# Binary search for top-k limits with the sign inside the candidate, and all masks made ahead of the attention

## The chip, the cores and the metric

The kernel runs on one core of a Trainium2 chip. The metric is the device time of one execution in microseconds (us). The engines are TensorE (PE), VectorE (DVE), ScalarE (ACT), GpSimd (POOL), and SyncE (SP), which here issues the DMAs.

## The reference, cut to what matters

The program is one step of a two-layer decoder trunk for 1024 prompt tokens and 32 sample tokens (8 sequences of 4). Layer 0 is a sparse attention: an indexer scores every key for every query, the 256 best keys (129 for a sample token, out of 516) are kept, and the attention runs over these alone. Each sub-layer has adaLN parameters from a conditioning vector, and each layer ends in a SwiGLU feed-forward part.

```python
sc = einsum('bqsh,bqh->bqs', relu(dots), wi) * IDX_HEADS ** -0.5   # one score per query and key
sc = where(valid, sc, -inf)                                        # causal
_, sel = top_k(sc, 256)                                            # ties: the lower index wins
o = sparse_attend(q, k[sel], v[sel], sel <= qpos)                  # softmax over the kept keys
```

The kernel doesn't gather. It finds for each query the limit, which is the 256th largest score, and makes an additive mask with 0 for the kept keys and -1e30 for the others. Queries are handled in eight tiles of 128; tile i sees (i+1) x 128 keys. Tiles 0 and 1 have at most 256 keys and need no mask of this kind. So there are seven searches: tiles 2 to 7 and the sample tokens.

## The kernel before, in words

**Order of the stages.** Each engine has its own program, and the engines meet in semaphores. The first half of the projections and the indexer's scores come first. Then two things run side by side: on PE, ACT, POOL and SP the second half of the projections (`pe_proj_b`, `act_proj_b`, `pool_proj_b`, `sp_proj_b`); on DVE the search (`dve_select`, line 1587). Then comes the attention (`pe_att`, `dve_att`, `act_att`, `pool_att`), the output projection with the samples' attention, two feed-forward parts and the convolution layer.

**The second half of the projections** is a list of 39 items. Each is one product of PE into a PSUM bank (line 595), followed by a rotation product (L849) and by one chunk of the adaLN product (`pe_chunks`, L862), whose 512 KB of weights arrive in a ring `wraw` of four slots. The ring holds projection weights and adaLN chunks in one fixed order. SP issues the loads in that order (`sp_chunks` L755, `sp_weights` L745 and L746), and a load waits until the slot's last user is done: for a weight tile that is POOL's low part (`proj_lo`, L834), made behind ACT's high part (`proj_hi`, L828); for a chunk it is PE's product. In the first item of weight tile 8 (item 12), ACT makes the high parts of tiles 10 and 11. The adaLN chunk 14 takes the slot of tile 10. Behind that chunk, SP's queue has nine stores of `v_tok` (L807), the load of weight tile 12 and the load of chunk 15. ACT evacuates each product (L1005, or L1039 for the value tiles), POOL multiplies for the rotary part.

**The search.** The limit is found bit by bit over the 31 bits of the float's magnitude. In each round of the loop (`dve.Fori`) the scores of each of the seven tiles are compared with a candidate and counted. DVE counts five of them (L1600); ACT counts tiles 7 and 6, the two largest, with a Sign activation that sums up (`act_count`, L900). Small operations over two groups of columns then decide the bit: group 0 is the two tiles counted by ACT, group 1 the five others. Before the loop, a count at zero tells the sign of the limit of each row, and the scores are multiplied by that sign, so that the loop only searches positive numbers; behind the loop the limit and, tile by tile, the scores get the sign back. For the two tiles of ACT, whose Sign gives half a count for an equal score, a refinement of four passes each follows (L1675 to L1678).

**Where ACT counts.** ACT is in the items' order, so its counts have fixed places. `count_halves` (line 101) gives every item 10 units (the nine value items 3 to 11: 7 units), 363 in all, and each item two places, at its middle and its end. Count h of 64 (two a round) goes to the first place at or behind 24 + 4.9 h. On ACT, an item's first place is right behind the evacuation of its product, and the second is behind the rotation's evacuation, the high parts and the keys' evacuation.

**The masks.** Each mask takes six steps (`dve_mask_step`, line 1684): scores above the limit counted (L1694); how many equal ones are still to be kept (L1696) and which are equal (L1697); a running sum over these (L1699); the first ones kept (L1701); added to those above (L1703); turned to 0 and -1e30 (L1705). Step 0 also multiplies the scores by the sign (L1693). Every step waits for the one before. `dve_masks_at` puts the 42 steps between the first 28 of the attention's pairs, one and two in turns.

**The attention** runs over 64 pairs of heads (pair n works on tile n // 8). For a pair PE makes the scores (L1855), DVE adds the mask and takes the minimum (`dve_min`, L1942), ACT takes the exponential (L1986), DVE the reciprocal (L1949), POOL normalises (L2023), PE turns the probabilities (L1866) and multiplies the values (L1884). Three pairs are in flight. Forty more adaLN chunks run between the first 26 pairs on PE (L1897), through the same ring.

Of the kernel before, what the change touches and what calls it, by code (L numbers as in the profile page):

```python
# [32 lines left out]
KP = 256  # L33
# [317 lines left out]
def program(nc, x_prompt, x_sample, c_prompt, c_sample, cache_k, cache_v, cache_kidx, state_conv, page_table,  # L351
# [12 lines left out]
    with ExitStack() as ctx:  # L364
# [528 lines left out]
        def act_count(act, half):  # L893

            for h in range(64):
# [681 lines left out]

        def dve_select(dve, entries):
# [3 lines left out]
            cnt, ge, kk, sig, th, cand, inc = range(7)  # L1582
            held = {ge: 384, kk: 400, inc: 416}

            def v(j, a=0, b=E):

                return bank[5][:, held[j] + a:held[j] + b] if j in held else bv[:, BS + E * j + a:BS + E * j + b]

            def vi(j, a=0, b=E):
                return v(j, a, b).bitcast(I32)  # L1590

            one = lambda r, j: v(r, j, j + 1)
            ka = bank[5][:, 432:432 + NA]
            groups = ((0, NA), (NA, E))

            def count(j, threshold):
# [3 lines left out]
                return dve.tensor_scalar(junk(j, rows, L), s, at, 0.0, ALU.is_ge, ALU.add,  # L1600
                                         accum_out=one(cnt, j)[0:rows])
# [3 lines left out]
            link(dve, dve.memset(bv[:, BS:BS + 7 * E], 0.0))  # L1605
            for j in range(E):
                ins = count(j, 0.0)
            link(dve, ins)
            for j, (s, rows, L, k) in enumerate(entries):
                ins = dve.tensor_scalar(one(ge, j), one(cnt, j), float(k), None, ALU.is_ge)  # L1610
# [6 lines left out]
            for j, (s, rows, L, k) in enumerate(entries):  # L1617
                if j < NA:
                    dve.tensor_scalar(ka[:, j:j + 1], one(kk, j), -2.0, float(L), ALU.mult, ALU.add)
# [1998 lines left out]
```

## Time and profile before

| | |
|---|---|
| median of three runs | 2630.7 us (2629.5 to 2631.8) |
| the profiled execution | 2635.3 us, span 2633.5 us |
| PE busy | 2512.0 us, 95% of the span |
| DVE busy | 1771.3 us, 67% |
| POOL busy | 1287.4 us, 49% |
| ACT busy | 1101.9 us, 42% |

The span goes from the first to the last instruction. PE's matmuls are pipelined and their ends are modelled. The chain that ended last is followed back from the last instruction, at each step to what released it. In the stretch of the change, the search loop runs from 199.4 to 373.8 us, the attention's first product starts at 383.0, and the masks are made from 386.9 to 480.5.

### The profile page before, as it was taken

What the parts mean: (1) busy time and instruction counts of PE and PEld (TensorE: products, weight loads), DVE (VectorE), ACT (ScalarE), POOL (GpSimd) and SP (SyncE); (2) the same over time, 40 slices, a digit from 0 to 9 for tenths busy, and PEclk for the clock granted to TensorE, in tenths of its full rate; (3) what the DMA queues carried; (4) which work ended last, traced back from release to release, by engine and by line L of the source; (5) the groups of instructions that cost most, each with busy time, mean ns of one, the idle gap of its engine ahead of it and who ended that gap; (6) DMA issues with size and microseconds to landing.
All of it is one profiled execution on the core that took longest, in us unless ns stands there. A gap on an engine that the chain in (4) does not pass through costs nothing.

```text
span 2633.5 us, 51699 instructions
## 1 busy us (share of the span) xinstructions
PE 2512.0 (95%) x20164; PEld 2312.3 (88%) x20164; DVE 1771.3 (67%) x3137; ACT 1101.9 (42%) x2061; POOL 1287.4 (49%) x967
## 2 busy tenths in 40 slices
PE   6979999999998999999999989999989999999999
PEld 4848874677798999999999989999989999999999
DVE  6388888665347756656567687767785665656775
ACT  5155656775235444344212343332454444442223
POOL 3404652344134656566544545545455656654454
PEclk7999999999999999999999999999999999999999
DMA  9205557201433435344894333328334534469731
GB/s 322 78 21 153 177 207 255 70 2 68 129 113 101 146 124 164 117 155 139 328 349 167 117 98 106 107 82 328 117 98 131 164 117 155 139 207 366 278 131 70
DMA packets 316390, 408.00 MB, mean 155 GB/s; under 512 B 40816, under 2 KB 227032, under 8 KB 313338
## 3 DMA queue, kind: packets, MB, share of 16 engines
q1 hardware_dynamic: 316154, 404.75, 45.9%
q8 instruction: 161, 2.64, 0.4%
q14 instruction: 75, 0.61, 0.1%
HBM read 284.85 MB, written 119.85 MB: 154 GB/s over the span
## 4 chain that ended last, share of the span: by engine, by line
PE 70%; DVE 11%; DMA 6%; issue 5%; POOL 4%; ACT 2%; SPq 2%; ACTq 0%; DVEq 0%; POOLq 0%
PE PS L595 10%; PE PS L2492 9%; PE PS L2494 9%; PE PS L2493 9%; PE PS L2553 5%; PE PS L2555 5%; PE PS L2556 5%; PE PS L1855 3%; PE PS L1884 2%; PE PS L1866 2%; POOL ring L2864 2%; DMA t_scratch<-stage 2%; DMA a_scratch<-stage 1%; POOL stage L2877 1%; DVE s_all L1552 1%
## 5 line engine op out<-in xcount | busy, mean ns | idle before, releaser
L2492 PE MATMUL PS<-th,ring 128*128 128x264 f32 x2800 | 800.2, 286 | 19.9 <-DVE y L3007 8.2
L2494 PE MATMUL PS<-th,ring 128*128 128x264 f32 x2800 | 796.8, 285 | 0.0
L2493 PE MATMUL PS<-th,ring 128*128 128x264 f32 x2800 | 795.9, 284 | 0.0
L2492 PEld LDWEIGHTS PS<-th,ring 128*128 128x128 f32 x2800 | 527.8, 189 | 26.8 <-issue 26.1
L2493 PEld LDWEIGHTS PS<-th,ring 128*128 128x128 f32 x2800 | 528.0, 189 | 0.0
L2494 PEld LDWEIGHTS PS<-th,ring 128*128 128x128 f32 x2800 | 527.9, 189 | 0.0
L2864 POOL TENSOR_TENSOR ring<-wraw,ring 128x512 fp32r<-128x512 f32 x232 | 340.3, 1469 | 368.1 <-ACT ring L2648 367.8
L2864 POOL TENSOR_TENSOR ring<-sums,ring 128x512 fp32r<-128x512 f32 x216 | 322.2, 1493 | 276.3 <-ACT ring L2648 276.3
L2553 PE MATMUL PS<-th,ring 128*128 128x264 f32 x1232 | 354.8, 288 | 14.3 <-DVE zs L3196 6.7
L2555 PE MATMUL PS<-th,ring 128*128 128x264 f32 x1232 | 352.9, 286 | 0.0
L2556 PE MATMUL PS<-th,ring 128*128 128x264 f32 x1232 | 352.5, 286 | 0.0
L2648 ACT ACTIVATE ring<-wraw 128x512 fp32r<-128x512 f32 x340 | 211.8, 626 | 299.2 <-PE PS L2556 168.2
L3193 DVE SCALAR_TENSOR_TENSOR y<-PS,mod,y 128x528 f32<-128x528 f32 x308 | 235.0, 766 | 141.2 <-PE PS L2556 128.0
L3007 DVE TENSOR_TENSOR y<-y,PS 128x528 f32<-128x528 f32 x150 | 104.9, 699 | 293.8 <-PE PS L2494 293.6
L2648 ACT ACTIVATE ring<-sums 128x512 fp32r<-128x512 f32 x216 | 136.1, 631 | 353.2 <-PE PS L2494 173.3
L2553 PEld LDWEIGHTS PS<-th,ring 128*128 128x128 f32 x1232 | 234.4, 190 | 16.1 <-issue 11.7
L2556 PEld LDWEIGHTS PS<-th,ring 128*128 128x128 f32 x1232 | 234.7, 191 | 0.0
L2555 PEld LDWEIGHTS PS<-th,ring 128*128 128x128 f32 x1232 | 234.6, 190 | 0.0
L2877 POOL TENSOR_TENSOR stage<-y,stage 128x528 fp32r<-128x528 f32 x110 | 179.2, 1629 | 77.3 <-ACT stage L2668 77.3
L595 PE MATMUL PS<-hhi,uhi 128*128 128x352 f32 (+1 forms) x552 | 189.0, 342 | 14.5 <-DVE hlo L1267 7.3
L2696 ACT ACTIVATE y<-PS 128x528 f32<-128x528 f32 x173 | 105.1, 607 | 186.4 <-PE PS L2494 185.3
L595 PE MATMUL PS<-hhi,ulo 128*128 128x352 f32 (+1 forms) x552 | 180.8, 328 | 0.0
(393 smaller groups left out, 5164.4 us busy)
## 6 DMA issues: line engine op xcount, KB each, us to landing
t_scratch<-stage SPq DMA_DIRECT2D x154, 528.0 KB, 3.3
th<-t_scratch SPq DMA_DIRECT2D x77, 1056.0 KB, 8.7
wraw<-in_ffn_w_gu_dram SPq DMA_DIRECT2D x96, 512.0 KB, 5.2
wraw<-in_ada_w_dram SPq DMA_DIRECT2D x80, 512.0 KB, 4.8
wraw<-in_ffn_w_down_dram SPq DMA_DIRECT2D x80, 256.0 KB, 5.9
wraw<-in_conv_w_in_dram SPq DMA_DIRECT2D x28, 512.0 KB, 5.3
y<-y_scratch SPq DMA_DIRECT2D x12, 1056.0 KB, 8.9
y_scratch<-y SPq DMA_DIRECT2D x6, 2112.0 KB, 7.9
```

Of the source, the lines that this page charges most:

```text
L595: last = pe.matmul(out, w(kt), x(kt), start=(n == 0), stop=(n == 3 * count - 1))
L2492: pe.matmul(out, hi, x[:, TH, k, :], start=(k == 0 and i in (1, 2, 5)), stop=False, skip_group_check=True)
L2493: pe.matmul(out, hi, x[:, TL, k, :], start=False, stop=False, skip_group_check=True)
L2494: last = pe.matmul(out, lo, x[:, TH, k, :], start=False, stop=(k == 3), skip_group_check=True)
L2553: pe.matmul(out, hi, x[:, TH, 2 * k + s, :], start=(k == 0 and i in (1, 2, 5)), stop=False, skip_group_check=True)
L2555: pe.matmul(out, hi, x[:, TL, 2 * k + s, :], start=False, stop=False, skip_group_check=True)
L2556: last = pe.matmul(out, lo, x[:, TH, 2 * k + s, :], start=False, stop=(k == 1), skip_group_check=True)
L2648: act.activation(slot_of(p)[:, RH, :], split_source(p), ACT.Copy).then_inc(w_hi, 1)
L2696: act.activation(out, result(r, it.groups), ACT.Silu if it.kind == "g" and pos == 6 else ACT.Copy).then_inc(rd_a, 1)
L2864: pool.tensor_tensor(w[:, RL, :], split_source(p), w[:, RH, :].bitcast(F32), ALU.subtract).then_inc(w_lop, 1)
L2877: pool.tensor_tensor(lo.rearrange("p (s n) -> p s n", s=2), token_part(v, i), hi.rearrange("p (s n) -> p s n", s=2), ALU.subtract).then_in ...
L3193: ins = dve.scalar_tensor_tensor(out=out, in0=result(r, BOTH), scalar=gate_of(f, m)[:, 0:1], in1=out, op0=ALU.mult, op1=ALU.add)
```

## The change

**The search.** The candidate is a float with its sign. The count at zero gives its first value, 2.0 or -1.9999998807907104, the number before -2 in magnitude, and each round flips bits of it with exclusive or. The scores are no longer multiplied by a sign. The columns are ordered anew (`COL`), so that tiles 7, 6 and the samples are columns 0 to 2 and tiles 2, 5, 4 and 3 columns 3 to 6. A round has five counts, one behind the other, and then five small operations behind them; before, it had seven, three of them between the counts. There are 31 rounds instead of 32.

**Where ACT counts.** There are 62 counts, and count h goes to the first place at or behind 12 + 4.3 h.

**Behind the loop.** One small operation over the limits of ACT's tiles becomes four, and the last four become three; the refinement's passes stay, with an addition in place of a maximum.

**The masks.** All 42 steps run ahead of the attention (`dve_masks_first`), with `relu` as scratch in place of `mscr`; none is left between pairs. The step that gives the scores their sign back is gone.

```diff
-    return [next(s for s, t in enumerate(at) if t >= 24 + 4.9 * h) for h in range(64)]
+    return [next(s for s, t in enumerate(at) if t >= 12 + 4.3 * h) for h in range(62)]
...
-            for j, (s, rows, L, k) in enumerate(entries):
-                dve.tensor_scalar(one(kk, j), one(ge, j), float(2 * k - L - 1), float(L - k + 1), ALU.mult, ALU.add)
-                ins = dve.tensor_scalar(one(sig, j), one(ge, j), 2.0, -1.0, ALU.mult, ALU.add)
-            link(dve, ins)
-            for j, (s, rows, L, k) in enumerate(entries):
-                if j < NA:
-                    dve.tensor_scalar(ka[:, j:j + 1], one(kk, j), -2.0, float(L), ALU.mult, ALU.add)
-                dve.tensor_scalar(s, s, one(sig, j)[0:rows], None, ALU.mult)
-            ins = dve.memset(v(cand), 2.0)
+            for a, b, k in ((0, 2, KP), (2, 3, KS), (3, E, KP)):
+                dve.tensor_scalar(v(th, a, b), v(cnt, a, b), float(k), 2.0, ALU.is_ge, ALU.mult)
+                ins = dve.tensor_scalar(v(cand, a, b), v(cnt, a, b), float(k), -1.9999998807907104, ALU.is_lt, ALU.mult)
+            link(dve, ins)
+            ins = dve.tensor_tensor(v(cand), v(cand), v(th), ALU.add)
...
+            with dve.Fori(0, ROUNDS) as i:
+                dve.wait_ge(sel, i * 6 + base)
+                count(2, None, ALU.is_ge)
+                dve.wait_ge(cand_rdy, i + 1)
+                signal(count(6, None, ALU.is_lt))
+                count(3, None, ALU.is_ge)
+                count(4, None, ALU.is_ge)
+                signal(count(5, None, ALU.is_ge))
+                dve.wait_ge(sel, i * 6 + (base + 1))
                 dve.wait_ge(sign_cnt, i * NA + NA)
+                signal(dve.tensor_tensor(v(lt, 0, 3), v(cnt, 0, 3), v(kk, 0, 3), ALU.is_gt))
+                dve.wait_ge(sel, i * 6 + (base + 2))
+                signal(dve.tensor_scalar(vi(inc, 3), v(cnt, 3), float(KP), bv[:, bass.ds(i + BITF, 1)], ALU.is_lt, ALU.mult))
+                dve.wait_ge(sel, i * 6 + (base + 3))
+                signal(dve.tensor_scalar(vi(inc, 0, 3), v(lt, 0, 3), bv[:, bass.ds(i + BITF, 1)], None, ALU.mult))
+                dve.wait_ge(sel, i * 6 + (base + 4))
+                signal(dve.scalar_tensor_tensor(out=vi(cand, 3), in0=vi(inc, 3), scalar=bvi[:, bass.ds(i + (BITI + 1), 1)],
+                                                in1=vi(cand, 3), op0=ALU.bitwise_xor, op1=ALU.bitwise_xor))
+                dve.wait_ge(sel, i * 6 + (base + 5))
+                dve.scalar_tensor_tensor(out=vi(cand, 0, 3), in0=vi(inc, 0, 3), scalar=bvi[:, bass.ds(i + (BITI + 1), 1)],
+                                         in1=vi(cand, 0, 3), op0=ALU.bitwise_xor, op1=ALU.bitwise_xor).then_inc(cand_rdy, 1)
...
-            link(dve, dve.tensor_tensor(v(cand), v(th), v(sig), ALU.mult))
...
-                link(dve, dve.tensor_scalar(s, s, bv[0:rows, BS + 3 * E + j:BS + 3 * E + j + 1], None, ALU.mult))
...
+        MASKS_FIRST, MASKS_LATE = (2, 5, 4, 3, 1, 0, 6), ()
+
+        def dve_masks_first(dve, entries):
+
+            for j in MASKS_FIRST:
+                for step in range(6):
+                    dve_mask_step(dve, entries, j, step, relu)
             dve.wait_ge(ki_stored, 32)
 
         def dve_masks_at(dve, entries, n):
 
-            for x in range(3 * n // 2, 3 * (n + 1) // 2 if n < 28 else 0):
-                dve_mask_step(dve, entries, (2, 5, 4, 3, 1, 0, 6)[x // 6], x % 6)
+            if 2 <= n < 2 + 6 * len(MASKS_LATE):
+                dve_mask_step(dve, entries, MASKS_LATE[(n - 2) // 6], (n - 2) % 6, mscr)
```

## Rows read from the trace of the kernel before

**Rows 1.** The page: its first line, and the chain that ended last by engine.

```profile
span 2633.5 us, 51699 instructions
...
PE 70%; DVE 11%; DMA 6%; issue 5%; POOL 4%; ACT 2%; SPq 2%; ACTq 0%; DVEq 0%; POOLq 0%
```

**Rows 2.** Timeline, PE: start, duration (us), engine, line, out<-in, [idle before <-releaser].

```profile
382.97 0.49 PE L1855 MATMUL PS<-kT,hhi 64*128 64x128 f32 x4 [0.54 <-ACT mod L889]
384.75 0.49 PE L1855 MATMUL PS<-kT,hhi 64*128 64x128 f32 x4 [1.29 <-DVE bv L1942]
```

**Rows 3.** Timeline, DVE: the end of the counts at zero, and one round.

```profile
193.22 0.53 DVE L1610 TENSOR_SCALAR PS<-bv 128x1 f32<-128x1 f32 x7
...
226.58 0.61 DVE L1600 TENSOR_SCALAR_CACHE_REDUCE junkB<-s_all,bv 128x384 bf16<-128x384 f32 x1
...
229.91 0.73 DVE L1600 TENSOR_SCALAR_CACHE_REDUCE junkC<-s_smp,bv 32x516 bf16<-32x516 f32 x1
...
230.69 0.17 DVE L1636 TENSOR_TENSOR PS<-bv,PS 128x5 f32<-128x5 f32 x1
230.89 0.23 DVE L1638 TENSOR_SCALAR PS<-PS,bv 128x5 int32<-128x5 f32 x1
231.16 0.22 DVE L1640 SCALAR_TENSOR_TENSOR bv<-PS,bv 128x5 int32<-128x5 int32 x1
...
231.56 0.61 DVE L1600 TENSOR_SCALAR_CACHE_REDUCE junkB<-s_all,bv 128x384 bf16<-128x384 f32 x1
```

**Rows 4.** Timeline, ACT: a count of tile 7, the evacuation of item 30, count 51.

```profile
336.39 1.15 ACT L900 ACTIVATE junkA<-s_all,bv 128x1024 bf16<-128x1024 f32 x1 [1.59 <-DVE bv L1640]
...
338.19 0.46 ACT L1005 ACTIVATE psgB<-PS 128x352 f32<-128x352 f32 x1 [0.55 <-PE PS L595]
338.55 1.03 ACT L900 ACTIVATE junkA<-s_all,bv 128x896 bf16<-128x896 f32 x1
```

**Rows 5.** Timelines of ACT, POOL, SP and PE, 241 to 259 us.

```profile
241.52 1.04 ACT L900 ACTIVATE junkA<-s_all,bv 128x896 bf16<-128x896 f32 x1
...
242.55 2.00 ACT L828 ACTIVATE uhi<-wraw 128x1024 fp32r<-128x1024 f32 x2
...
243.68 4.75 POOL L834 TENSOR_TENSOR ulo<-wraw,uhi 128x1024 fp32r<-128x1024 f32 x2 [1.02 <-ACT uhi L828]
...
252.37 3.15 SPq L755 DMA_DIRECT2D wraw<-in_ada_w_dram  x3
...
258.46 0.64 PE L862 MATMUL PS<-wraw,cT 128*32 128x256 f32 x8 [2.08 <-DMA wraw<-in_ada_w_dram]
```

**Rows 6.** Timeline, DVE, from the end of the loop to the first pair.

```profile
373.84 0.18 DVE L1670 SCALAR_TENSOR_TENSOR bv<-bv 128x2 f32<-128x2 f32 x1
374.05 0.75 DVE L1675 TENSOR_SCALAR relu<-s_all,bv 128x1024 f32<-128x1024 f32 x1
...
382.84 0.17 DVE L1679 TENSOR_TENSOR PS<-bv,PS 128x2 f32<-128x2 f32 x1
...
383.43 0.72 DVE L1682 TENSOR_TENSOR bv<-bv 128x7 f32<-128x7 f32 x1
384.18 0.29 DVE L1942 CUSTOM_DVE_ANT_0 PbS<-PS,cneg 128x128 f32<-128x128 f32 x1
```

**Rows 7.** DVE on the masks' scratch (window, length, busy), and line 1696 (ns).

```profile
386.90:485.00 98.10, 37.90 (x49) 0.95 0.76 251
...
L1696 DVE TENSOR_SCALAR bv<-bv x7: 136/149/150, 390.2 to 471.2; 128x1 f32<-128x1 f32 x6, 32x1 f32<-32x1 f32 x1
```

**Rows 8.** Waits of PE, 383 to 500 us: total us, times, longest.

```profile
PE PS L1866 <- POOL PbS L2023: 3.3, 5, 1.2
PE PS L1897 <- DMA wraw<-in_ada_w_dram: 2.6, 4, 1.1
```

**Rows 9.** Windows: length, busy of PE, PEld, DVE, ACT, POOL, PE's clock, DMA share, GB/s.

```profile
386.00:397.00 11.00, 9.15 (x58) 3.84 (x58) 5.31 (x24) 3.86 (x20) 2.96 (x8) 0.53 0.94 350
```

**Rows 10.** The chain of waits, 383 to 460 us, its shares by line.

```profile
by line: DMA wraw<-in_ada_w_dram 28.7%; PE PS L1866 11.9%; PE PS L1897 11.9%; PE PS L1855 10.5%; DVE mscr L1699 7.9%; PE PS L1884 7.9%; issue 7.6%; DVE PbS L1942 4.7%; DVE mscr L1697 2.7%; POOL PbS L2023 2.7%; DVE s_all L1693 2.2%; DVE bv L
```

More of the change, by code:

```diff
@@ L893, in act_count @@
         def act_count(act, half):
-            for h in range(64):
+            for h in range(62):
                 if COUNT_AT[h] == half:
@@ L1576, in link @@
             dve.wait_ge(sel, nsel[0])
+        COL = (0, 1, 3, 4, 5, 6, 2)
+        ROUNDS = 31
         def dve_select(dve, entries):
             E = len(entries)
[L1582 to L1596, printed above, removed]
+            cnt, lt, kk, low, th, cand, inc = range(7)
+            held = {lt: 384, kk: 400, inc: 416}
+            tiny = 1.1754943508222875e-38
+            def v(r, a=0, b=E):
+                return bank[5][:, held[r] + a:held[r] + b] if r in held else bv[:, BS + E * r + a:BS + E * r + b]
+            def vi(r, a=0, b=E):
+                return v(r, a, b).bitcast(I32)
@@ L1598, in count, with one @@
+            def one(r, j):
+                return v(r, COL[j], COL[j] + 1)
+            def count(j, threshold, op):
                 s, rows, L, _ = entries[j]
                 at = threshold if isinstance(threshold, float) else one(cand, j)[0:rows]
-                return dve.tensor_scalar(junk(j, rows, L), s, at, 0.0, ALU.is_ge, ALU.add,
-                                         accum_out=one(cnt, j)[0:rows])
+                return dve.tensor_scalar(junk(j, rows, L), s, at, 0.0, op, ALU.add, accum_out=one(cnt, j)[0:rows])
@@ L1603, in dve_select, with signal @@
+            def signal(ins):
+                ins.then_inc(sel, 1)
             dve.wait_ge(smp_rdy, 1)
             dve.wait_ge(score_rdy, 8 * len(TILES))
-            link(dve, dve.memset(bv[:, BS:BS + 7 * E], 0.0))
+            link(dve, dve.memset(v(cnt), 0.0))
             for j in range(E):
-                ins = count(j, 0.0)
+                ins = count(j, 0.0, ALU.is_ge)
+            for j in range(NA):
+                dve.memset(one(kk, j), float(entries[j][2] - 2 * entries[j][3]))
+            dve.memset(one(kk, E - 1), float(entries[E - 1][2] - entries[E - 1][3]))
@@ new lines, in dve_select @@
+            nsel[0] += 6 * ROUNDS
+            dve.wait_ge(sel, nsel[0])
+            dve.wait_ge(cand_rdy, ROUNDS + 1)
+            dve.scalar_tensor_tensor(out=v(inc, 0, NA), in0=v(cand, 0, NA), scalar=tiny, in1=v(cand, 0, NA),
+                                     op0=ALU.is_ge, op1=ALU.mult)
+            link(dve, dve.tensor_scalar(v(lt, 0, NA), v(cand, 0, NA), 0.0, -tiny, ALU.is_lt, ALU.mult))
+            link(dve, dve.tensor_tensor(v(low, 0, NA), v(cand, 0, NA), v(lt, 0, NA), ALU.min))
+            link(dve, dve.tensor_tensor(v(th, 0, NA), v(inc, 0, NA), v(low, 0, NA), ALU.add))
@@ L1688, in dve_mask_step @@
             out = mask_s[0:rows, :] if j == 6 else mask_of((7, 6, 2, 5, 4, 3)[j])
[L1689 to L1691 removed]
+            A, B = scratch[0:rows, 0, 0:L], scratch[0:rows, 1, 0:L]
+            t = bv[0:rows, BS + 5 * E + COL[j]:BS + 5 * E + COL[j] + 1]
+            n = bv[0:rows, BS + COL[j]:BS + COL[j] + 1]
             if step == 0:
[L1693 removed]
                 link(dve, dve.tensor_scalar(A, s, t, 0.0, ALU.is_gt, ALU.add, accum_out=n))
@@ L3536, in _ @@
             dve_select(dve, entries)
-            dve_masks_first(dve)
+            dve_masks_first(dve, entries)
             dve_att(dve, entries)
```

58 lines of the change are left out of this document (6 added, 52 removed).

## The prediction, made before the change was run

> **What bounds the kernel now.** I read the page first: the span is 2633.5 us and TensorE (PE) carries 70% of the chain that ended last, VectorE (DVE) 11% [rows 1]. So a change on DVE counts only where PE waits for it. Next, PE's timeline where the projections hand over to the attention: PE's first score product of the attention runs at 382.97 and ends by 383.46, and the second waits 1.29 us for DVE, to 384.75 [rows 2]. DVE starts the first pair's minimum at 384.18 [rows 6]. Search and PE arrive almost together there; DVE is the later by 0.7 us, so a later end of DVE's work moves all behind it one for one. Then DVE's rounds [rows 3], ScalarE's (ACT's) counts between the evacuations of PE's products [rows 4], the one stall of PE in the projections [rows 5], DVE's work behind the rounds [rows 6], the masks' cost [rows 7], and what PE waits for in the first 28 pairs [rows 8].
>
> **The search, alone on DVE.** A round takes 4.98 us (226.58 to 231.56) [rows 3]. To the start of the fifth count are 3.33 us, four counts and four small operations; seven small ones that don't wait for each other take 0.53 at 193.22, so four with a register's operand some 0.4. The fifth count and its read-out take 0.78 more (to 230.69), 0.68 without the signal. Five counts: 3.33 - 0.4 + 0.68 = 3.6. The old tail is a chain of four small operations. In the new one, every small operation stands behind the five counts in two interleaved chains; the last to matter is: signal of the sum (0.1), increment to candidate (0.27, as 230.89 to 231.16), candidate to the next round (a step like it, 0.28): 0.65. New round 4.26. The preparation loses the sign's operations and the passes that multiply the scores: the counts at zero end at 193.22 [rows 3], and with some 1.4 for the fifteen small ones the loop may start at 194.6. 31 rounds of 4.26 would end at 326.7.
>
> **The search with ACT.** They don't end there. Tiles 7 and 6 are counted on ACT, at fixed places of its program, and the round waits for both. Count h stands at the first half-item at or behind 12 + 4.3h on the list of half-items. The last, h = 61, wants 274.3 and gets 278, the first half of item 30. Before, h = 51 wanted 24 + 4.9 x 51 = 273.9 and got the same place. So its row is there: behind the evacuation at 338.19, the count runs from 338.55 for 1.03 us [rows 4]. DVE can go on at 339.7; 0.5 to the last candidate and 0.25 for it to be seen give 340.4, 33.4 before the 373.84 of the old loop. DVE's own rounds have 13 us to spare, so ACT's places are the bound.
>
> **A stall that grows.** PE sits 2.08 us before the product at 258.46, for an adaLN chunk issued at 252.37 [rows 5]. SP was late with it, because an earlier chunk of its queue needs the slot of weight tile 10, free only when POOL has made its low part (243.68, two tiles in 4.75 us), behind ACT's high part at 242.55. Before, one count stands ahead of that (at 241.52). Now two do, h = 19 and h = 20, both on the first half of item 12, and h = 20 needs the candidate that h = 19 decides: 19 ends near 242.2, DVE's answer takes 0.8, the count of tile 7 takes 1.15 [rows 4], so the high part starts at 244.2. All of the queue behind (nine stores, a weight load, the chunk) shifts by 1.65 us, and PE's stall with it. Every later item, the last count among them, comes 1.65 later: 342.0. The projections then end at 385.1 on PE, which costs nothing by itself, DVE being later. I take it whole; bounds 0 and 3.3 (twice that, if the late evacuation of item 13, 1.9 us behind its product, holds PE as well).
>
> **Behind the loop.** The one limit operation becomes four in a row of about 0.2 (373.84 to 374.05 is such a step): 0.7 in all. The two refinement blocks keep their eight passes, 374.05 to 382.84, 8.8. The end has three small steps instead of four, 0.6, and loses the 0.72 operation over seven columns at 383.43 [rows 6]; I take it as gone, and if something else caused that time, it stays: 0 to 0.6. Limits at 352.1.
>
> **The masks.** All instructions that touch the masks' scratch take 37.9 us, with seven one-column operations of 0.15 [rows 7]: 38.9. Each of some 42 starts when the one before has signalled, 0.03 to 0.04 later: 40.5. The seven multiplications by the sign (already apart from this) are gone. 352.1 + 40.5 = 392.6 against 384.18: **8.4 us later**. It is on the path in full, since nothing of the attention but the first score product can run before.
>
> **What comes back.** Between pairs PE waited 3.3 us for POOL's normalising, five times, the longest 1.2 in the filling of the pipeline [rows 8]. The other 2.1 sit behind long mask steps, as DVE's reciprocal comes after them. I take 2.1 back. The 2.6 for adaLN chunks I leave: with a ring of four slots a load starts only when PE has used a chunk, so it moves with PE. Bounds 0 and 4.7. Outside these two, PE had work in these pairs, and a quicker DVE gives nothing.
>
> **The clock.** PE's granted clock is at 0.53 from 386 to 397 [rows 9], the lower of its two levels (1.2 and 2.4 GHz) nearly all the time, after PE idled in the hand-over. With 8 us more of idleness it will be low already for the second and third score products (0.49 at the full clock [rows 2], at most as much again): 0.3 more each is my estimate, 0.6 in all. Bounds -1 and +2. The Trainium skill (TensorE: Matmul & The Clock Gate, Part 1: The HAM clock gate) says that the array falls to the lower level when it has been idle; by that alone the longer idleness costs whatever work newly falls in the low stretch, and the 0.6 would be paid. The trace agrees with the direction; how much this change adds no row shows.
>
> **The sum.** 8.4 + 0.6 - 2.1 = +6.9 us. The profiled execution took 2635.3 (span 2633.5 and 1.8 around it), so its like would take 2642.2; it lies 4.6 above the median of 2630.7, and the difference is added to the median: **2637.6 us**, slower by 0.26%.
>
> **Rivals.**
> 1. *Not slower: the masks between pairs were dearer than PE's idle time says.* The chain from 383 to 460 has DVE's scan, compare and sign steps on 7.9 + 2.7 + 2.2% of 77 us, 9.9 us [rows 10]. If all of it comes back in place of 2.1, the sum is 8.4 + 0.6 - 9.9 = -0.9: 2629.8. It decides from 9 us on. For it: the chain. Against: a chain passes through DVE also where PE works beside it, and PE's waits there add up to 4.7 at most. 0.13.
> 2. *No further stall.* The slot of tile 10 comes free as before, or the chunk lands sooner: 1.65 less, 2636.0. For it: I derive the order of two counts, no row shows it. 0.17.
> 3. *DVE's round is the bound.* More waits on register values a round could make it as long as before: 194.6 + 31 x 4.98 = 349.0 against 341.3 for the last small operations, 7.7 more: 2645.3. For it: eight such waits instead of seven. Against: five small operations instead of seven, and the old round's time is accounted for by its operations. 0.08.
> 4. *The placement doesn't hold the search, or the masks are cheaper back to back, so that DVE is ready before PE.* Then 0.7 and 2.1 are won: 2627.9. It needs 9 us that I don't find. 0.07.
>
> **Chances.** The forecast 0.55, with its own range 2634.5 to 2641. A difference of under 0.2% (5.3 us) can't be told from none: the bounds are 2625.4 and 2636.0. Slower: 0.45 of the forecast's, half of rival 2, rival 3: 0.6. Faster: small parts of rivals 1 and 4: 0.06. Same: the rest. The range reaches from rival 1 at the low end to the forecast with a doubled stall and no give-back at the upper one: 2629 to 2642.
>
> **What would show it.** Right: the last count on ACT at 340.0 to 340.4; PE's stall near 260 at 3.7; 40 us of mask steps in one block from 352; PE idle about 8 us before the second score product, near 393; no wait for POOL over 0.2 behind the filling. Wrong: a round on DVE of over 4.8 without a wait for ACT; the first minimum before 388; PE's waits in the first 28 pairs falling by much more than 2 us, or the pairs 0 to 27 taking over 5 us less from the first minimum on.

## The result, and the profile of the changed kernel

The changed kernel takes 2658.9 us in the median of four runs (2656.0 to 2664.2), the kernel before 2631.3 beside it (2629.5 to 2635.0): a ratio of 1.0095, with a 95% interval of 1.0072 to 1.0119. The forecast was 2637.6 in a range of 2629 to 2642. The ratio is +25 us (19 to 31), the two medians stand 27.6 apart, and the forecast was +6.9: the sign was right, the size off by a factor of three to four. Beside the later kernels of this study the kernel before took 2635.6 to 2637.3 in the median, which is why all comparisons go by ratios.

The page of the changed kernel, its first line and the chain by engine (before: [rows 1]):

```profile
span 2656.4 us, 51551 instructions
...
PE 64%; DVE 15%; issue 7%; DMA 5%; POOL 4%; ACT 3%; SPq 2%; DVEq 0%; ACTq 0%; POOLq 0%
```

PE's share of the chain fell from 70% to 64%, DVE's rose from 11% to 15%. Next, who PE waits for from 383 to 500 us (total us, times, longest; before: [rows 8]):

```profile
PE PS L1842 <- DVE bv L1929: 22.2, 2, 21.5
PE PS L1853 <- POOL PbS L2010: 1.3, 2, 1.1
PE PS L1853 <- ACT PT L1980: 0.5, 1, 0.5
```

The reader sees both halves of the forecast's balance. The waits for POOL fell from 3.3 to 1.3 and those for adaLN chunks from 2.6 to nothing, more than the 2.1 that I had counted back. Against it stands one wait of 21.5 us for DVE; I had written 8. DVE's timeline has the first count, the end of the loop (the first operation behind it), the block of masks and its end:

```profile
184.47 1.22 DVE L1603 TENSOR_SCALAR_CACHE_REDUCE junkA<-s_all 128x1024 bf16<-128x1024 f32 x1
...
344.29 0.17 DVE L1651 SCALAR_TENSOR_TENSOR PS<-bv 128x2 f32<-128x2 f32 x1
...
355.85 0.61 DVE L1676 TENSOR_SCALAR_CACHE_REDUCE relu<-s_all,bv 128x384 f32<-128x384 f32 x1
...
403.88 0.29 DVE L1929 CUSTOM_DVE_ANT_0 PbS<-PS,cneg 128x128 f32<-128x128 f32 x1
```

The first minimum comes at 403.88, against 384.18 before [rows 6] and 392.6 in the forecast. The difference of the two profiled spans, 22.9 us, splits so:

| stretch | before | changed | difference | forecast |
|---|---|---|---|---|
| start to the first minimum | 384.2 | 403.9 | +19.7 | +8.4 |
| first minimum to the last product of the values | 266.5 | 267.3 | +0.8 | -1.5 |
| the rest | 1982.9 | 1985.3 | +2.4 | 0 |

The last line is no effect of the change: over the fourteen kernels of this study, whose rest is the same program, it lay between 1979.8 and 1991.6.

The first line understates the miss, because the two profiled executions didn't start alike. DVE's first count stands at 184.47 in the changed kernel; before it stood 3.2 us later:

```profile
187.66 1.22 DVE L1600 TENSOR_SCALAR_CACHE_REDUCE junkA<-s_all 128x1024 bf16<-128x1024 f32 x1
```

Over all kernels it stands between 184.3 and 189.8, and PE and ACT move with it. So I count from there. The first minimum comes 219.4 us behind the first count, 196.5 before and 204.9 in the forecast: 22.9 later instead of 8.4. The 14.5 us by which this misses are made of three pieces: the loop ended 159.8 us behind the first count instead of 154.3 (+5.5), the work behind it took 11.6 instead of 10.1 (+1.5), and the masks 48.0 instead of 40.5 (+7.5).

### The profile page after: what moved, and what is told of

The parts are those of the page before. It is cut to its first block, busy times and chain, and to the rows that moved or that the text cites. A ratio compares the mean times of both kernels' runs of the same rounds, so it can differ in the third digit from the quotient of the medians.

```text
span 2656.4 us, 51551 instructions
## 1 busy us (share of the span) xinstructions
PE 2516.3 (95%) x20164; PEld 2313.4 (87%) x20164; DVE 1763.3 (66%) x3000; ACT 1100.0 (41%) x2057; POOL 1290.7 (49%) x967
## 4 chain that ended last, share of the span: by engine, by line
PE 64%; DVE 15%; issue 7%; DMA 5%; POOL 4%; ACT 3%; SPq 2%; DVEq 0%; ACTq 0%; POOLq 0%
PE PS L2479 9%; PE PS L2481 9%; PE PS L2480 9%; PE PS L2540 5%; PE PS L2542 4%; PE PS L2543 4%; PE PS L595 4%; PE PS L1842 3%; PE PS L1871 3%; PE PS L1853 2%; POOL ring L2851 2%; DMA t_scratch<-stage 2%; DMA a_scratch<-stage 1%; POOL stage L2864 1%; DVE junkA L1603 1%
## 5 line engine op out<-in xcount | busy, mean ns | idle before, releaser
L2540 PEld LDWEIGHTS PS<-th,ring 128*128 128x128 f32 x1232 | 233.2, 189 | 16.3 <-issue 12.1
```

What stands on the lines that cost most here:

```text
L2540: pe.matmul(out, hi, x[:, TH, 2 * k + s, :], start=(k == 0 and i in (1, 2, 5)), stop=False, skip_group_check=True)
```

## Why the round is longer: the tail, and what stands in it

A round of the changed kernel, on DVE:

```profile
226.43 0.61 DVE L1603 TENSOR_SCALAR_CACHE_REDUCE junkB<-s_all,bv 128x384 bf16<-128x384 f32 x1 [0.32 <-issue]
...
230.04 0.15 DVE L1636 TENSOR_TENSOR PS<-bv,PS 128x3 f32<-128x3 f32 x1
230.27 0.23 DVE L1638 TENSOR_SCALAR PS<-bv 128x4 int32<-128x4 f32 x1
230.40 0.22 DVE L1640 TENSOR_SCALAR PS<-PS,bv 128x3 int32<-128x3 f32 x1
230.64 0.22 DVE L1642 SCALAR_TENSOR_TENSOR bv<-PS,bv 128x4 int32<-128x4 int32 x1
230.78 0.21 DVE L1645 SCALAR_TENSOR_TENSOR bv<-PS,bv 128x3 int32<-128x3 int32 x1
231.31 0.61 DVE L1603 TENSOR_SCALAR_CACHE_REDUCE junkB<-s_all,bv 128x384 bf16<-128x384 f32 x1 [0.32 <-issue]
```

The counts take 3.61 (226.43 to 230.04), as worked out. The tail takes 1.27, from 230.04 to 231.31, and I had given it 0.65. The steps are uneven: 0.23, 0.13, 0.24, 0.14, and then 0.53 to the next count, 0.32 of it "issue", time in which the engine waited for nothing that the profile shows. Before, the tail was 0.87, from 230.69 to 231.56 [rows 3]: four small operations, three of them a chain, and the turn. (The old round has eight small operations, four between the counts and four behind them, not seven as I had counted.) DVE waited for ACT in 3 of the 31 rounds only, 2.1 us in all, so this round, 4.88, is the bound. Two theories: (A) DVE's sequencer is the bound, for each wait on a register's value and the loop's turn are work of its own, more of which stands bare behind the counts now than before; (B) it is the time from one dependent small operation to the next.

**The loop taken away.** With it go all register values: the columns of the bit tables, `bass.ds(i + ...)`, become constants too.

```diff
-            with dve.Fori(0, ROUNDS) as i:
+            for i in range(ROUNDS):
```

> The 31 rounds of the search stand one behind the other, without a loop, so every wait and every column is a constant and nothing is computed in a register. Same counts, same small operations, same waits. Theory A (the tail of a round is bound by what DVE's sequencer does between operations: register values for waits and columns, and the loop's turn): the tail falls from 1.28 to 0.65 to 0.9, the round from 4.89 to 4.3 to 4.5, and the first minimum comes 12 to 18 us earlier; ACT's last count at 340 then comes into play. Rival B (the tail is the time from one small operation's end to the next one's start through a semaphore, whatever the sequencer does): the round stays at 4.8 to 4.9 and the time within 3 us of the changed kernel's 2658.9.

```profile
226.44 0.15 DVE L1636 TENSOR_TENSOR PS<-bv,PS 128x3 f32<-128x3 f32 x1
226.54 0.23 DVE L1638 TENSOR_SCALAR PS<-bv 128x4 int32<-128x4 f32 x1
226.68 0.22 DVE L1640 TENSOR_SCALAR PS<-PS,bv 128x3 int32<-128x3 f32 x1
226.81 0.22 DVE L1642 SCALAR_TENSOR_TENSOR bv<-PS,bv 128x4 int32<-128x4 int32 x1
226.94 0.21 DVE L1645 SCALAR_TENSOR_TENSOR bv<-PS,bv 128x3 int32<-128x3 int32 x1
227.07 0.60 DVE L1603 TENSOR_SCALAR_CACHE_REDUCE junkB<-s_all,bv 128x384 bf16<-128x384 f32 x1
```

The same operations and the same dependencies, with constants for registers: a step of 0.10 to 0.14, a tail of 0.63, a round of 4.24 (227.07 to 231.31). The forecast's 4.26 was right for a tail without register work, and theory A holds: the dependencies alone don't make the tail. By the rows, 0.40 of the 0.64 us between the two tails stand in the turn (0.53 for 0.13) and 0.24 in the four steps. Whether it is the waits, the columns taken from a register or the branch, this run doesn't say. The time is 2653.8, ratio 1.0060 (1.0036 to 1.0083). The mean of 30 rounds, though, is 4.78, not 4.24: now ACT's places are the bound, as forecast: DVE waits for ACT in 13 of the rounds, 16.3 us. The last round is one of them:

```profile
341.26 0.07 DVE L1603 DVE_READ_ACCUMULATOR junkA<-s_all,bv 128x1 f32 x1
341.95 0.17 DVE L1636 TENSOR_TENSOR PS<-bv,PS 128x3 f32<-128x3 f32 x1 [0.62 <-ACT junkA L900]
...
342.75 0.50 DVE L1651 SCALAR_TENSOR_TENSOR PS<-bv 128x2 f32<-128x2 f32 x1
```

ACT's last count starts at 340.72 and the loop ends at 342.75; the forecast's two numbers were 340.2 and 342.0. So the step on the placement was worked out right, for a round that the loop did not have.

**More waits, in the tail and between the counts.** Three more waits a round, on a value long reached:

```diff
 (in the tail: ahead of the three middle small operations)
                 dve.wait_ge(sel, i * 6 + (base + 2))
+                dve.wait_ge(cand_rdy, i + 1)
 (between: ahead of each of the last three counts)
+                dve.wait_ge(cand_rdy, i + 1)
                 count(3, None, ALU.is_ge)
```

> Three more waits a round, each on a value computed from the loop's register and long reached when it is looked at, put ahead of three of the five small operations in the tail. Theory A: each costs what a register's operation and a wait cost in the open, 0.05 to 0.2, so the tail grows by 0.15 to 0.6 and the search by 5 to 18 us. Rival B: nothing, the waits lie inside the time that an operation needs anyway; the round stays at 4.89.

> The same three further waits a round as in the run with waits in the tail, but ahead of the last three counts, where the running count of 0.6 to 0.8 us can cover them. Theory A: the round stays at 4.89 (plus 0.1 at most). If waits on register values cost wherever they stand, it grows as much as with the waits in the tail.

With the waits in the tail, the small operations stand at 227.19, 227.42, 227.61, 227.90, 228.04 and the next count at 228.57: the tail is 1.38 instead of 1.27, the round 4.98. So three such waits cost 0.11 together, less than the 0.15 that I had as the lower end, and waits of this kind don't explain the 0.64. Between the counts they cost nothing: 228.20 to 233.07, a round of 4.87. The end-to-end ratios, 1.0085 (1.0067 to 1.0102) and 1.0083 (1.0066 to 1.0100), can't tell 3 us apart; the traces can.

**Small operations back between the counts.** The chain of columns 0 to 2 is moved between the counts, as in the kernel before; two operations stay behind the fifth (the waits move with them and are left out here, as are the lines removed).

```diff
                 count(3, None, ALU.is_ge)
+                signal(dve.tensor_tensor(v(lt, 0, 3), v(cnt, 0, 3), v(kk, 0, 3), ALU.is_gt))
                 count(4, None, ALU.is_ge)
+                signal(dve.tensor_scalar(vi(inc, 0, 3), v(lt, 0, 3), bv[:, bass.ds(i + BITF, 1)], None, ALU.mult))
                 signal(count(5, None, ALU.is_ge))
+                dve.scalar_tensor_tensor(out=vi(cand, 0, 3), in0=vi(inc, 0, 3), scalar=bvi[:, bass.ds(i + (BITI + 1), 1)],
+                                         in1=vi(cand, 0, 3), op0=ALU.bitwise_xor, op1=ALU.bitwise_xor).then_inc(cand_rdy, 1)
```

> The three small operations' chain of the tiles counted first (columns 0 to 2: comparison, increment, candidate) stands between the counts, as far as ACT's count is there; two small operations are left behind the fifth count. 31 rounds and the sign in the candidate stay. Theory A: the operations between counts cost 0.1 to 0.2 each beside their own waits being hidden, the tail falls to 0.8 to 0.9, the round to 4.5 to 4.65, and the search ends 7 to 12 us earlier, if ACT's count of the round is not late in the middle of the round. Rival B: two dependent steps fewer in the tail, but three more between the counts: 4.7 to 4.9.

The round is 4.74 (229.15 to 233.89). The tail is still 0.93, of which 0.55 is the loop's turn, and it didn't reach the 4.65 of theory A: the turn stays bare. The 0.15 a round didn't shorten the search, which I had expected to end 7 to 12 us earlier: the whole loop took 154.4 us (193.26 to 347.61), 153.3 in the changed kernel (191.00 to 344.29), because DVE now waits for ACT in 5 rounds, 6.6 us. The ratio is 1.0069 (1.0052 to 1.0086).

**How much of the result the tail is.** This needs two executions that start alike. The run with the counts placed otherwise (below) has the slow tail and its first count at 187.9, and the run without the loop has it at 188.0. The loop ends at 347.38 in the one and at 342.75 in the other:

```profile
347.38 0.17 DVE L1651 SCALAR_TENSOR_TENSOR PS<-bv 128x2 f32<-128x2 f32 x1
```

The tail costs 4.6 us. Counted from the first count (159.8 against 154.8) it is 5.0 in the changed kernel's own profile. That is rival 3's mechanism (register waits make DVE's round the bound), at 4.88 instead of the 4.98 it assumed. I gave it 0.08. Of the 4.6, 2.8 reach the first minimum (406.99 against 404.19): without the loop the work behind it is 0.8 shorter, but the masks start earlier and stand beside POOL for longer (its work ends at 391 there), so that they take 50.7 us, 353.51 to 404.19, where both the changed kernel and the one with the counts placed otherwise take 48.0.

## Why the masks take 48.0 us: POOL beside them

Steps of one kind and size don't take the same time in the block. Here are the mask of tile 3 in the changed kernel, and POOL's work at that time:

```profile
361.26 0.15 DVE L1678 TENSOR_SCALAR bv<-bv 128x1 f32<-128x1 f32 x1
361.45 1.10 DVE L1679 TENSOR_SCALAR relu<-s_all,bv 128x512 f32<-128x512 f32 x1
362.59 1.23 DVE L1681 TENSOR_TENSOR_SCAN relu<-relu 128x512 f32<-128x512 f32 x1
363.85 0.75 DVE L1683 SCALAR_TENSOR_TENSOR relu<-relu,bv 128x512 f32<-128x512 f32 x1
364.64 1.31 DVE L1685 SCALAR_TENSOR_TENSOR relu<-s_all,bv,relu 128x512 f32<-128x512 f32 x1
365.99 1.05 DVE L1687 TENSOR_SCALAR masks<-relu 128x512 bf16<-128x512 f32 x1
```

```profile
361.33 0.95 POOL L1119 TENSOR_TENSOR qst_<-qcB,pafB 128x352 f32<-128x352 f32 x1
364.15 1.26 POOL L1106 TENSOR_TENSOR qcB<-psgB,ropeC 128x352 f32<-128x352 f32 x1 [1.87 <-ACT psgB L1005]
365.36 1.41 POOL L1113 TENSOR_TENSOR pafB<-pafB,ropeS 128x352 f32<-128x352 f32 x1
```

The step of 1.23 has no POOL operation beside it. The compare of 1.10 started inside one of POOL's (361.33 to 362.28) and ends 0.27 behind it. The step of 0.75 was there first: POOL's next operation starts inside it, at 364.15, and it is POOL's that takes 1.26 for 0.94. The step of 1.31 started inside that one, and the one of 1.05 inside POOL's next, which takes 1.41. So in these rows the one that comes second waits. The theories: (C) the two engines hold each other up; (D) the steps are slow because of the new scratch or because they stand back to back.

**The same block with POOL idle.**

```diff
+            dve.wait_ge(fin_rdy, 45)
             for j in MASKS_FIRST:
```

> The masks wait until GpSimd (POOL) has done its last work of the projections (near 386 in the changed kernel); nothing else is changed. Theory C (the mask steps are slowed by POOL's own operations beside them): the 42 steps take 40 to 41 us instead of 48.0, none longer than in the kernel before, so the first minimum is near 427 and the kernel 20 to 24 us slower than the changed one. Rival D (the steps are slow because of the other scratch buffer, or because they stand back to back): they take 48 again, first minimum near 434.

```profile
384.91 0.61 DVE L1676 TENSOR_SCALAR_CACHE_REDUCE relu<-s_all,bv 128x384 f32<-128x384 f32 x1 [29.18 <-POOL xn L1119]
...
389.89 0.49 DVE L1679 TENSOR_SCALAR relu<-s_all,bv 128x512 f32<-128x512 f32 x1
390.41 1.23 DVE L1681 TENSOR_TENSOR_SCAN relu<-relu 128x512 f32<-128x512 f32 x1
391.67 0.75 DVE L1683 SCALAR_TENSOR_TENSOR relu<-relu,bv 128x512 f32<-128x512 f32 x1
392.46 0.75 DVE L1685 SCALAR_TENSOR_TENSOR relu<-s_all,bv,relu 128x512 f32<-128x512 f32 x1
...
425.61 0.29 DVE L1930 CUSTOM_DVE_ANT_0 PbS<-PS,cneg 128x128 f32<-128x128 f32 x1
```

The block takes 40.7 us, 384.91 to the first minimum at 425.61, in the same scratch and back to back: 40.5 was the forecast. The compare of 512 columns is back at 0.49, the sum of two inputs at 0.75. And POOL, now alone, does its seventeen operations from 359 to 385 in 0.93 to 0.95 each. Theory C holds, D is out. Row by row it adds up: twelve of the changed kernel's steps are longer than the same ones here, by 0.5 to 0.7 each and 7.2 together, and all others are equal to 0.01. The ratio is 1.0143 (1.0117 to 1.0169); the wait costs more than POOL's company. Of the pieces of the miss, 7.3 us are this, and the 1.5 behind the loop as well: there the two additions (L1660) took 1.85 and 1.73 us, where they came second, and 1.23 and 1.09 in the run without the loop, where POOL had nothing beside them; the first compare took 1.03 for the 0.75 of [rows 6].

Which steps suffer is to be seen in the rows: those with a scalar operand and no sum (L1659, L1679, L1687), and those with two inputs (L1660, L1683, L1685, the scan L1681). Those that also sum up (L1676: 0.75 in both kernels) and the reduction (L1661: 1.22) never do, in any of the fourteen profiles. That is why the loop, all counts, ran at its old speed beside the same POOL and gave no warning. The Trainium skill says this (SBUF — State Buffer, "SBUF: two separate sides"): VectorE and GpSimd share a pair of ports that whichever starts first holds for the whole instruction, when VectorE runs in a mode that uses both its ports, or reads two inputs from SBUF against a GpSimd operation that reads SBUF, and "the other fully blocks"; the section "Who interferes with whom" takes out the form that writes its accumulator, and the reduction. The traces agree in every row above, with 0.3 to 0.7 us for a step of DVE that comes second. I had taken the durations from [rows 7] and not asked who runs beside the block.

**The old search, masks ahead.** The other half of the change alone: the 42 steps moved ahead of the attention in the kernel before, in its own scratch.

```diff
         def dve_masks_first(dve, entries):
+            for x in range(42):
+                dve_mask_step(dve, entries, (2, 5, 4, 3, 1, 0, 6)[x // 6], x % 6)
```

> The kernel before, with its own search and its own scratch, but all seven masks ahead of the attention: the other half of the change alone. POOL has ended its work of the projections by then (386), so theory C expects 42 to 43 us for the block (40.5 and the seven multiplications by the sign, about 0.5 each), and the first minimum at 426 to 428. If the steps were slow because they stand back to back (rival D), it is 50. PE idles for over 40 us. The kernel takes 35 to 42 us more than the one before, so the two halves of the change do not add up from their own times: the new search alone gives about nothing, and with the masks ahead it is worth 15 to 20.

The block runs from 383.09 to 428.77, 45.7 us: 40.7 and 5.0 for the seven multiplications, of which the first, 384 columns beside POOL's last work, takes 1.16 and one of 512 columns, without POOL, 0.48. The ratio is 1.0173 (1.0149 to 1.0196), about 46 us: more than expected. Against it the new search with the same masks ahead is 20 us faster.

**The new search, masks between the pairs.**

```diff
-        MASKS_FIRST, MASKS_LATE = (2, 5, 4, 3, 1, 0, 6), ()
+        MASKS_FIRST, MASKS_LATE = (), (2, 5, 4, 3, 1, 0, 6)
...
-            if 2 <= n < 2 + 6 * len(MASKS_LATE):
-                dve_mask_step(dve, entries, MASKS_LATE[(n - 2) // 6], (n - 2) % 6, mscr)
+            for x in range(3 * n // 2, 3 * (n + 1) // 2 if n < 28 else 0):
+                dve_mask_step(dve, entries, MASKS_LATE[x // 6], x % 6, mscr)
```

> The new search alone: all seven masks are made between the attention's pairs as in the kernel before, one and two steps in turns. The difference to the changed kernel is the price of making them ahead. DVE has its limits near 356, 27 us before PE's first score product, so the first minimum comes right behind that product, near 383 to 384. By my account (the loss is masks on the path, and the clock behind them) the kernel takes 2627 to 2631, no slower than before and up to 3 us faster. If the new search costs something elsewhere (the counts on ACT at earlier places), it stays over 2636.

```profile
389.77 0.29 DVE L1929 CUSTOM_DVE_ANT_0 PbS<-PS,cneg 128x128 f32<-128x128 f32 x1 [27.53 <-PE PS L1842]
```

Ratio 0.9999 (0.9985 to 1.0013): the new search alone neither costs nor gains. The 27.5 us by which its limits are there earlier all go into waiting for PE. So the whole loss is the masks' place, and the two halves together are not the sum of their own effects: 0 and +46 make +25.

## Why nothing came back: the clock

PE's granted clock by stretch (length, PE's busy time, clock, DMA share, GB/s), changed kernel:

```profile
384.00:404.00 20.00, 0.00 (x0) 0.51 0.45 169
404.00:414.00 10.00, 7.29 (x44) 0.50 0.17 48
414.00:424.00 10.00, 10.00 (x66) 0.50 0.70 228
424.00:434.00 10.00, 10.00 (x66) 0.60 0.71 231
```

PE idles for 21.5 us, the clock goes to its lower level (1.2 of 2.4 GHz), and stays there for 29 us of the attention, until 433, with PE busy all the time from 414 on. Before, it was low for 10 us [rows 9]. A scores product takes 0.80 there instead of 0.49, sixteen matmuls of the adaLN chunks 1.93 instead of 1.07.

**PE kept busy while it waits.** Transposes of the identity, whose results nobody reads, behind the first score product:

```diff
             for n in range(LA):
                 pe_scores(pe, n)
+                if n == 0:
+                    for x in range(130):      (190 in the second run)
+                        pe.transpose(bank[7][:, 0:P], ident[:], ident[:])
```

> PE gets 130 transposes of the identity into an unused PSUM bank, whose result nobody reads, behind its first score product of the attention, so that it isn't idle for the 21.5 us in which DVE makes the masks. Theory E (the changed kernel's attention gave nothing back because PE's clock fell in that idle time and stayed low for 47.8 us in all, 27 of them under work): the granted clock stays at 1.0 from 383 to 431, the stretch from the first minimum to the last product of the values takes 261 to 263 us instead of 267.0, and the kernel 4 to 6 us less than the changed one. Rival F (the clock isn't what costs there; the attention is slow for its DMAs or POOL): the same 266 to 267.

> As the run with 130 transposes, with 190, whose result nobody reads: they take 21 us and so fill PE's idle time to its end near 404 (130 left 7.9 us idle, and the clock fell in these). Theory E: the granted clock stays at 1.0 past the first minimum, at most 5 us of work at the lower level instead of 29, and from the first minimum to the last product of the values it takes 259 to 262 us (267.3 in the changed kernel, 264.8 with 130). Rival F: 264 to 267 with a clock of 1.0.

With 130, PE is busy to 397 and idle for 7.9 us, and the clock is low for 14 us of the attention; with 190 (same view as above):

```profile
384.00:404.00 20.00, 19.46 (x177) 1.00 0.58 211
404.00:414.00 10.00, 5.99 (x44) 0.73 0.00 0
414.00:424.00 10.00, 9.32 (x82) 0.76 0.75 245
424.00:434.00 10.00, 9.21 (x90) 1.00 0.89 314
```

The clock is at its full level for all of the wait. It falls all the same, in the first pairs, where PE has only 6 us of work in 10: I put that dip down to the filling of the pipeline, as the kernel before has one of the same length, 10 us. From the first minimum to the last product of the values it takes 264.8 and 263.3 us, where the changed kernel has 267.3. I expected 259 to 262. So in these executions the clock is worth 2.5 to 4 us, less than the 4 to 6 I gave it, and the ratios can't tell it: 1.0098 (1.0076 to 1.0121) and 1.0077 (1.0054 to 1.0099). Over all runs whose masks are ahead of the attention, the time at the low level behind the first minimum, from windows of 1 us, goes with the attention's length:

| kernel | low, us | attention, us |
|---|---|---|
| old search, masks ahead | 9.0 | 263.5 |
| counts placed | 9.9 | 261.0 |
| PE busy, 190 | 10.2 | 263.3 |
| waits in the tail | 11.5 | 261.7 |
| PE busy, 130 | 14.4 | 264.8 |
| unrolled | 15.3 | 265.7 |
| after POOL | 20.5 | 266.9 |
| between the counts | 20.6 | 264.9 |
| waits between | 28.9 | 267.2 |
| changed | 29.1 | 267.3 |

A line through them rises by 0.25 us an us, with a scatter of 1 to 2 us that the clock doesn't explain. All executions on record agree on the slope: in 115 of them, each held against the mean of its own kernel, 1 us more at the lower level over the whole program (from the mean granted clock) goes with 0.29 us more of time. That is a correlation; it doesn't say in which stage.

The length of the low stretch isn't set by the idle time alone: with 19 to 23 us of idleness ahead, six kernels have 10 (counts placed), 12 (waits in the tail), 15 (unrolled), 21 (between the counts) and 29 (waits between, changed), and the two with over 40 have 9 and 21 (unrolled and after POOL in two pieces). What decides is open. The 29 isn't an odd case for the changed kernel: its mean granted clock is 0.978 in the profiled execution and 0.974 to 0.981 in all four.

What the masks' absence between the pairs gives back can't be read as closely as I had hoped. At 10 us low, as before, the attention takes 261.0 to 263.5 against 266.5 in the kernel before. But the new search with all masks between the pairs takes 263.3, with 7 us low, and differs in the attention only by the seven multiplications that it leaves out. Against the first it would be 3 to 5.5 us, against the second 3 at most and perhaps nothing. The 2.1 that I counted lies inside that, and it was paid away to the clock in this execution.

The Trainium skill (TensorE: Matmul & The Clock Gate, Part 1: The HAM clock gate) says the array starts fast again after a short time of work. In the changed kernel it had 19 us of unbroken work (414 to 433) at the low level; the trace doesn't agree, neither by the granted clock nor by the products of 0.80, and the trace decides.

## The stall of PE in the projections

In the changed kernel PE waits for two chunks:

```profile
250.13 0.64 PE L862 MATMUL PS<-wraw,cT 128*32 128x256 f32 x8 [3.31 <-DMA wraw<-in_ada_w_dram]
...
257.87 0.64 PE L862 MATMUL PS<-wraw,cT 128*32 128x256 f32 x8 [0.92 <-DMA wraw<-in_ada_w_dram]
```

4.2 us against 2.08 [rows 5] and 3.7 forecast. The cause was read as two counts ahead of the high parts in item 12.

```diff
-    ... if t >= 12 + 4.3 * h) for h in range(62)]
+    ... if t >= 14 + 4.3 * h) for h in range(62)]
```

> The changed kernel with count h at 14 + 4.3 h instead of 12 + 4.3 h: then one count instead of two stands ahead of the high parts in item 12, all else nearly in place (the last count stays in item 30). The prediction's step on the stall says that PE's wait for the adaLN chunk near 250 to 260 falls from 4.2 to about 2.1 us. As DVE's work is the later at the hand-over, PE's gain shows as idle time there: the time stays within 2 us of the changed kernel's. If two counts there are not the reason, the wait stays at 3.5 to 4.2.

The high parts follow the evacuation after 1.4 us (241.44 to 242.81), where the changed kernel takes 4.8 (237.17 to 241.94); that part of the reading is right. (In the changed kernel the second of the two counts waits 2.15 us for DVE's answer, where the forecast had 0.8.) But the stall is 0.8 + 2.4 = 3.2, between the two predictions. And nine other kernels with the changed kernel's places have 3.2 to 5.6, the version below, with the places of this run, 1.8. The stall differs between executions by as much as the effect looked for, so the share of the two counts isn't settled. It costs nothing here: ratio 1.0086 (1.0063 to 1.0109). It would where PE is the later. Behind the first count, PE's first score product comes after 195.3 us before and after 199.4 with the new search and all masks between the pairs, where the stalls add up to 5.6.

## A version that beats both

Four masks fit into the time in which DVE would wait for PE. First that alone, then with the unrolled loop and the counts at 14 + 4.3 h:

```diff
-        MASKS_FIRST, MASKS_LATE = (2, 5, 4, 3, 1, 0, 6), ()
+        MASKS_FIRST, MASKS_LATE = (2, 5, 4, 3), (1, 0, 6)
```

> The four smaller masks of the prompt (tiles 2, 5, 4 and 3) ahead of the attention, the three of tiles 6, 7 and the samples between pairs 2 to 19, one step each. The four take 22 us by their share of the elements, up to 26 beside POOL: from 356 to 378 to 382, which ends before PE's first score product, or with it. First minimum near 383 to 384, and fewer waits between pairs than with all masks there: 2625 to 2630. If the block is stretched further it comes at 386 to 388, and the kernel is level with the one before.

> The best that the runs point to: the 31 rounds without a loop, the counts at 14 + 4.3 h, the masks of tiles 2, 5, 4 and 3 ahead of the attention and the other three between pairs 2 to 19. DVE ends the four masks near 378, before PE's first score product, so nothing of the masks is on the path there. PE's stall in the projections falls by 2 us, and the waits for POOL and for chunks between the pairs by up to 3. Against the kernel before: 2 to 6 us less, 2626 to 2635 beside a before of 2631 to 2637. If what PE gains in the projections is lost to the clock or to the chunks in the attention, it is level with it.

The split alone is level with the kernel before: 0.9998 (0.9982 to 1.0014). Its last mask ends with the score product that DVE waits for otherwise:

```profile
381.88 1.18 DVE L1687 TENSOR_SCALAR masks<-relu 128x768 bf16<-128x768 f32 x1
383.09 0.29 DVE L1929 CUSTOM_DVE_ANT_0 PbS<-PS,cneg 128x128 f32<-128x128 f32 x1
```

PE waits 0.9 us for DVE and 1.6 for POOL's last rotary product, which the masks delay. All three edits together take 2628.2 us in the median of twelve runs, beside 2635.6 of the kernel before: 0.9972 (0.9959 to 0.9985), some 7 us. DVE's timeline of this kernel:

```profile
375.44 1.18 DVE L1687 TENSOR_SCALAR masks<-relu 128x768 bf16<-128x768 f32 x1
380.40 0.29 DVE L1929 CUSTOM_DVE_ANT_0 PbS<-PS,cneg 128x128 f32<-128x128 f32 x1 [3.79 <-PE PS L1842]
```

DVE has 3.8 us to spare at the hand-over though its steps are stretched by POOL, the wait for POOL is gone, and PE's wait for a chunk is 1.8 us instead of 4.1. Behind the first count, the first minimum comes after 196.1 us, after 198.7 in the split alone and after 196.5 before. The two last edits weren't tried apart in this setting, and both can have a part: in the split alone DVE was the later by some 0.2 us, and without the loop and the stall PE and DVE both come earlier. So which of them brings the gain is open, and so is where the 7 us against the kernel before are won: the profiled execution, 2632.6, is one of the slower of the twelve and 2.7 below that of the kernel before, which started 3.4 us later.

## Why the prediction was wrong, point by point

- **What bounds the hand-over** (a later end of DVE's work counts one for one): right.
- **The counts**, 3.6 us: right, 3.61. The old round's small operations were eight and not seven, which the sum for the counts didn't use, only the argument against rival 3.
- **The tail of the round**, 0.65: wrong, 1.27. I took steps of rows 3 for the last links of the chain and nothing for the register work and the turn of a tail that now holds every small operation. Unrolled it is 0.63. With it DVE's round is the bound, and the loop ends 4.6 to 5.0 us later than ACT's places allow.
- **ACT's places as the bound**: right only without the loop (342.75 against 342.0).
- **The stall**, 3.7: 4.2, its cause half shown, off the path. Rival 4 forgot it: if DVE were ready first, PE's own arrival, 1.65 later, would count, and its 2627.9 would be 2629.6.
- **Behind the loop**, 10.1: 11.6, by three passes beside POOL.
- **The masks**, 40.5: wrong, 48.0. This step failed most. The durations came from a stretch without POOL's rotary work (its last product ends at 385, the masks begin at 386.9) and with only short operations of POOL, 2.96 us in the first 11 [rows 9], and I moved them into one full of it. The cost that was taken as fixed was the duration of a step. Without POOL, 40.7.
- **The clock**, 0.6 with a bound of 2: too small; the low stretch was 19 us longer, which is 4.8 by the line above and 2.5 to 4 by the two runs with PE kept busy.
- **The give-back**, 2.1: not settled, between nothing and 5.5. With the clock it leaves the attention 0.8 us longer than before, where the forecast had 1.5 less.
- **The range** held each unknown by its nearest rows and none by a company that the step would newly have, so its upper end was 17 us too low.

## What to carry to other kernels

When work is moved, its durations don't move with it: look at what each other engine does in the new place, and for VectorE beside GpSimd ask of each instruction whether it has a second input or a plain scalar form. In a hardware loop, count what the sequencer does behind the last long operation; three waits a round cost nothing between the counts here and 0.11 us behind them. Moving work ahead of a hand-over pays up to the slack there and costs one for one beyond it, with the clock on top.

## What was not expected of the hardware

- The turn of a loop took DVE 0.53 us from the start of the last small operation to the next count, and 0.13 for the same code unrolled. It isn't a constant of the loop: in the kernel before, with another order of waits, it was 0.26 behind the last small operation and 0.40 behind the last one that waits. The register work ahead of the four other steps cost 0.24 together: 0.23, 0.13, 0.24 and 0.14 for 0.10, 0.14, 0.13 and 0.13.
- Three more such waits cost 0.11 together in the tail and nothing between counts of 0.6 to 0.9 us.
- Of DVE and POOL, the one that starts second is stretched. For DVE it is up to 0.7 us an instruction in the changed kernel: the last mask step of 384 columns 0.98 for 0.36, a scan of 768 columns 2.38 for 1.76. POOL's 0.94 grew to 1.80 there and to 2.52 in the run without the loop.
- PE's clock stayed at the lower level for 19 us of unbroken work in one execution and was back 8 us after the same wait's end in another (the run with the counts placed otherwise).
